# The recurrent mixer's inverses: the backward direction's U form in the other partition half, its products alternating with the forward's

## The reference

```python
def step(S, inp):
    r_t, w_t, k_t, v_t, kk_t, a_t = inp
    sa = jnp.einsum('dbhvk,dbhk->dbhv', S, kk_t)
    S = (S * w_t[..., None, :] - sa[..., :, None] * (kk_t * a_t)[..., None, :]
         + v_t[..., :, None] * k_t[..., None, :])
    return S, jnp.einsum('dbhvk,dbhk->dbhv', S, r_t)
_, ys = lax.scan(step, S0, seqs)
ys = jnp.moveaxis(ys, 0, 2)
y = ys[0] + jnp.flip(ys[1], axis=1)
```

## Time and profile before

| | us |
|---|---|
| median of 3 runs | 3585.34 |
| lowest, highest | 3580.81, 3586.29 |
| the profiled execution, its own time | 3579.05 |
| its span, first to last instruction | 3577.7 |
| TensorE busy | 3337.4 (93%) |
| VectorE busy | 1795.8 (50%) |
| ScalarE busy | 1114.4 (31%) |
| GpSimd busy | 267.2 (7%) |
| mean granted clock of TensorE | 0.972 |

### The profile page before, as it was taken

One profiled execution on the slowest core, in us unless ns is written; L12 is line 12 of the kernel. 1 busy time (PEld: TensorE's weight loads), 2 busy tenths in 40 slices (PEclk: granted clock), 3 DMA queues, 4 the chain that ended last, 5 costly groups with the idle time before them and its releaser, 6 DMA issues. The chain is left out here.

```text
span 3577.7 us, 55649 instructions
## 1 busy us (share of the span) xinstructions
PE 3337.4 (93%) x23830; PEld 2326.5 (65%) x23830; DVE 1795.8 (50%) x2790; ACT 1114.4 (31%) x1847; POOL 267.2 (7%) x218
## 2 busy tenths in 40 slices
PE   8989799998898997999989799889999999899999
PEld 6687543332667753333358688858888878688887
DVE  4655433322466443333245666476664562866735
ACT  3643300000355330000032433124333432743423
POOL 1011000000101100000020222301000100010001
PEclk9999999999999998999999899989999999999999
DMA  5131389999412217999962000012222222222222
GB/s 187 48 118 71 119 330 428 427 428 427 192 48 95 94 48 319 427 427 427 428 244 106 2 3 3 4 36 100 95 94 95 94 98 80 66 94 94 95 91 75
DMA packets 54389, 595.58 MB, mean 166 GB/s; under 512 B 5760, under 2 KB 10112, under 8 KB 16512
## 3 DMA queue, kind: packets, MB, share of 16 engines
q1 hardware_dynamic: 54144, 592.03, 41.2%
HBM read 589.91 MB, written 2.10 MB: 165 GB/s over the span
## 5 line engine op out<-in xcount | busy, mean ns | idle before, releaser
L683 PE MATMUL psum<-source_hi,weights_hi 128*128 128x512 f32 (+1 forms) x2352 | 922.6, 392 | 52.2 <-DVE weights_lo L570 36.4
L683 PE MATMUL psum<-source_lo,weights_hi 128*128 128x512 f32 (+1 forms) x2352 | 910.2, 387 | 0.0
L683 PE MATMUL psum<-source_hi,weights_lo 128*128 128x512 f32 (+1 forms) x2352 | 910.0, 387 | 0.0
L683 PEld LDWEIGHTS psum<-source_hi,weights_hi 128*128 128x128 f32 x2352 | 448.7, 191 | 154.8 <-DVE weights_lo L570 44.7
L570 DVE TENSOR_TENSOR weights_lo<-weight_ring,weights_hi 128x1024 fp32r<-128x1024 f32 (+4 forms) x321 | 350.8, 1100 | 320.3 <-ACT weights_hi L518 319.5
L683 PEld LDWEIGHTS psum<-source_lo,weights_hi 128*128 128x128 f32 x2352 | 448.9, 191 | 89.5 <-issue 3.4
L683 PEld LDWEIGHTS psum<-source_hi,weights_lo 128*128 128x128 f32 x2352 | 448.0, 190 | 88.5
L518 ACT CAST weights_hi<-weight_ring 128x1024 fp32r<-128x1024 f32 (+4 forms) x321 | 297.0, 935 | 614.0 <-PE psum L683 602.3
L1867 DVE TENSOR_TENSOR x<-psum,x 128x512 f32<-128x512 f32 x250 | 160.4, 684 | 207.2 <-PE psum L1714 207.2
L632 POOL TENSOR_TENSOR sums_of_squares<-squares 128x512 f32<-128x512 f32 (+1 forms) x17 | 27.7, 1629 | 2498.6 <-ACT squares L538 2498.6
L1678 PE MATMUL psum<-lent_weights,branches 128*64 128x512 f32 x800 | 182.1, 597 | 3.6 <-DMA lent_weights<-in_w_gate 2.5
(11 more groups left out here) (388 smaller groups left out, 4588.0 us busy)
## 6 DMA issues: line engine op xcount, KB each, us to landing
lent_weights<-in_w_down SPq DMA_DIRECT2D x26, 2048.0 KB, 18.5
lent_weights<-in_w_up SPq DMA_DIRECT2D x24, 2048.0 KB, 20.0
lent_weights<-in_w_gate SPq DMA_DIRECT2D x22, 2048.0 KB, 19.2
weight_ring<-in_ffn_w_up SPq DMA_DIRECT2D x22, 2048.0 KB, 7.7
weight_ring<-in_w_gate SPq DMA_DIRECT2D x20, 2048.0 KB, 16.3
weight_ring_first<-in_w_up SPq DMA_DIRECT2D x20, 2048.0 KB, 18.0
weight_ring<-in_w_up SPq DMA_DIRECT2D x16, 2048.0 KB, 20.8
weight_ring<-in_w_down SPq DMA_DIRECT2D x16, 2048.0 KB, 19.2
```

The lines of the kernel that those rows point to most:

```text
L683: ins = pe.matmul(ps, a, b, start=k == 0 and q == 0, stop=k == job.rows // P - 1 and q == 2)
```

## The change

Slots are renamed: U moves to slot `VAL`, Y and the early work's temporary to slot `GAMMA`. `far(d, h)` gives the partition half h for the forward direction and the other half for the backward one. The backward U, and the backward Y that belongs to it, now lie in the far half.

- Front: one more entry in `ops`, A's product again, written to the far half for the backward direction and copied through the mask of the first level; VectorE adds the identity, and that is U after level one. T's entry is masked with the first level at once, with the sign, and the identity added. `first_level` is gone.
- Inverses, TensorE: `together` issues a block of one direction and a block of the other, product by product; `alone` issues one block. T's update (forward) goes with Y's product (backward), and the next level's Y product (forward) with T's update (backward). U's updates stand alone. For the last level `move_back` makes the backward U in the near half: identity x U plus Y x U, accumulated in PSUM, which VectorE copies.
- Inverses, ScalarE: the last backward Y is copied with its sign turned; one `scale` of a level stands between the two copies.
- Inverses, VectorE: `mix` and `decay_sum` follow the updates of their direction, a level earlier than before.

```diff
 KAPPA, RHO, BETA, GAMMA, VAL, AT, BT, R1, R2, AM, VT, GT, BTT = range(13)
-T_INV, U_INV, Y_MAT = BETA, GAMMA, VAL
...
 I64, M_LT, M_GT, M_LE, M_GE, M_LEVEL = 0, 1, 2, 3, 4, 5
+M_FIRST = M_LEVEL, M_LEVEL + 6
...
+def far(d, h):
+
+    h = (h + d) % 2
+    return slice(HALF * h, HALF * h + HALF)
...
-        act.activation(self.w[d][:, VAL, :], self.x[d][:, XA, :], ACT.Identity, scale=self.col("rwkv_k_a_2"), bias=self.bias)\
+        act.activation(self.w[d][:, TEMP, :], self.x[d][:, XA, :], ACT.Identity, scale=self.col("rwkv_k_a_2"), bias=self.bias)\
...
@@ -2237,7 +2244,8 @@
     near = slice(0, HALF - 1), slice(1, HALF)
     edge = slice(0, 1), slice(HALF - 1, HALF)
 
-    ops = [(VT, None, None, None), (BTT, BETA, None, None), (AT, BETA, KAPPA, "strict"), (R1, BETA, RHO, "upto"),
+    ops = [(VT, None, None, None), (BTT, BETA, None, None), (AT, BETA, KAPPA, "strict"), (U_INV, BETA, KAPPA, "first"),
+           (R1, BETA, RHO, "upto"),
            (T_INV, KAPPA, BETA, "turned"), (GT, GAMMA, None, None), (BT, GAMMA, KAPPA, "strict"),
            (R2, GAMMA, RHO, "upto")]
     by_act = [kind is None for _, _, _, kind in ops]
@@ -2268,13 +2276,20 @@
                     r, s = slice(HALF * h, HALF * h + HALF), slice(n * HALF, (n + 1) * HALF)
                     lhs = val[d][r, s] if a is None else w[d][r, a, s]
                     rhs = w[d][r, b, s] if b is not None else c64(K, I64)[r, :]
-                    return pe.matmul(K.psum[r, 2 * (i % 4) + d, s], lhs, rhs, start=True, stop=True)
-
-                for n in range(NCH):
-                    op(0, 0, n)
-                    op(1, 1, n)
-                for n in range(NCH):
-                    last = op(0, 1, n), op(1, 0, n)
+                    to = far(d, h) if slot == U_INV else r
+                    return pe.matmul(K.psum[to, 2 * (i % 4) + d, s], lhs, rhs, start=True, stop=True)
+
+                if slot == U_INV:
+                    for n in range(NCH):
+                        op(0, 0, n)
+                        op(1, 0, n)
+                        last = op(0, 1, n), op(1, 1, n)
+                else:
+                    for n in range(NCH):
+                        op(0, 0, n)
+                        op(1, 1, n)
+                    for n in range(NCH):
+                        last = op(0, 1, n), op(1, 0, n)
                 for ins in last:
                     ins.then_inc(ready, 1)
 
@@ -2306,16 +2321,17 @@
                     if by_act[i]:
                         continue
                     dve.wait_ge(ready, 2 * i + d + 1)
-                    mask = {"strict": (M_LT, M_GT), "upto": (M_LE, M_GE), "turned": (M_GT, M_LT)}[kind][d]
-                    dve.scalar_tensor_tensor(out=chunks(w[d][:, Y_MAT if kind == "turned" else slot, :]),
-                                             in0=chunks(K.psum[:, 2 * (i % 4) + d, :]),
-                                             scalar=-1.0 if slot == R1 else 1.0, in1=over_chunks(c64(K, mask)),
+                    if slot == T_INV:
+                        dve.wait_ge(ready, 2 * i + 2)
+                    mask = {"strict": (M_LT, M_GT), "upto": (M_LE, M_GE), "turned": M_FIRST, "first": M_FIRST[::-1]}[kind][d]
+                    to = chunks(w[d][:, slot, :])
+                    dve.scalar_tensor_tensor(out=to, in0=chunks(K.psum[:, 2 * (i % 4) + d, :]),
+                                             scalar=-1.0 if slot in (R1, T_INV, U_INV) else 1.0, in1=over_chunks(c64(K, mask)),
                                              op0=ALU.mult, op1=ALU.mult).then_inc(kept, 1)
                     done += 1
-                    if kind == "turned":
+                    if slot in (T_INV, U_INV):
                         dve.wait_ge(kept, done)
-                        dve.wait_ge(ready, 2 * i + 2)
-                        link(first_level(K, dve, link, w[d], T_INV, Y_MAT))
+                        link(dve.tensor_tensor(to, to, over_chunks(c64(K, I64)), ALU.add))
 
...
+        near = lambda d, h: slice(HALF * h, HALF * h + HALF)
 
         @block.tensor
         def _(pe):
+
+            def of(d, bank, lhs, rhs, here, there):
+                def op(n, h):
+                    c = slice(n * HALF, (n + 1) * HALF)
+                    return pe.matmul(K.psum[there(d, h), bank + d, c], w[d][here(d, h), lhs, c], w[d][here(d, h), rhs, c],
+                                     start=True, stop=True)
+                return op
+
+            def y(d):
+                return of(d, 0, AM, T_INV, near, far)
+
+            def t(d):
+                return of(d, 4, U_INV, Y_MAT, far, near)
+
+            def u(d):
+                return of(d, 2, Y_MAT, U_INV, far, far)
+
+            def alone(op, sem):
+                for n in range(NCH):
+                    for h in range(2):
+                        ins = op(n, h)
+                ins.then_inc(sem, 1)
+
+            def together(op, sem, other, other_sem):
+                for n in range(NCH):
+                    op(n, 0)
+                    other(n, 0)
+                    last = op(n, 1), other(n, 1)
+                last[0].then_inc(sem, 1)
+                last[1].then_inc(other_sem, 1)
+
+            def move_back():
+                for n in range(NCH):
+                    c = slice(n * HALF, (n + 1) * HALF)
+                    for h in range(2):
+                        r, ps = far(1, h), K.psum[near(1, h), 3, c]
+                        pe.matmul(ps, c64(K, I64)[r, :], w[1][r, U_INV, c], start=True, stop=False)
+                        ins = pe.matmul(ps, w[1][r, Y_MAT, c], w[1][r, U_INV, c], start=False, stop=True)
+                ins.then_inc(u_upd, 1)
+
+            def await_level(m, d):
+                if m:
+                    pe.wait_ge(masked, 2 * (m - 1) + d + 1)
+                    pe.wait_ge(t_updated, 2 * (m - 1) + d + 1)
+
+            def await_y(m, d):
+                pe.wait_ge(y_kept, 2 * m + d + 1)
+                if m:
+                    pe.wait_ge(u_updated, 2 * (m - 1) + d + 1)
+
+            alone(y(0), y_ready)
             for m in range(levels):
-                for d in range(2):
-                    if m:
-                        pe.wait_ge(masked, 2 * (m - 1) + d + 1)
-                        pe.wait_ge(t_updated, 2 * (m - 1) + d + 1)
-                    heads(pe, d, 0, AM, T_INV, y_ready)
+                await_level(m, 1)
+                if m < levels - 1:
+                    await_y(m, 0)
+                    together(t(0), t_upd, y(1), y_ready)
+                else:
+                    alone(y(1), y_ready)
+                    await_y(m, 0)
+                alone(u(0), u_upd)
                 if early and m < 2:
                     if m:
                         pe.wait_ge(early.gates, 2)
                     early.low_rank(pe, m, 6)
-                for d in range(2):
-                    pe.wait_ge(y_kept, 2 * m + d + 1)
-                    if m:
-                        pe.wait_ge(u_updated, 2 * (m - 1) + d + 1)
-                    else:
-                        pe.wait_ge(u_begun, d + 1)
-                    if m < levels - 1:
-                        heads(pe, d, 4, U_INV, Y_MAT, t_upd)
-                    heads(pe, d, 2, Y_MAT, U_INV, u_upd)
+                await_y(m, 1)
+                if m < levels - 1:
+                    await_level(m + 1, 0)
+                    together(y(0), y_ready, t(1), t_upd)
+                if m < levels - 1:
+                    alone(u(1), u_upd)
+                else:
+                    move_back()
 
         @block.scalar
...
-                    act.copy(w[d][:, Y_MAT, :], K.psum[:, d, :]).then_inc(y_kept, 1)
+                    act.activation(w[d][:, Y_MAT, :], K.psum[:, d, :], ACT.Copy,
+                                   scale=-1.0 if d and m == levels - 1 else 1.0).then_inc(y_kept, 1)
+                    if early and m < 2 and d == 0:
+                        early.scale(act, 2 * m + 2)
                 if early and m < 2:
                     early.gate(act, m, 6)
-                    early.scale(act, 2 * m + 2)
                     early.scale(act, 2 * m + 3)
 
...
         def _(dve):
-            link = linker(dve, dlink)
-            for d in range(2):
-                first_level(K, dve, link, w[d], U_INV, AT).then_inc(u_begun, 1)
-            dve.wait_ge(u_begun, 2)
             for m in range(levels):
-                if early and m in (1, 2, 3):
-                    early.mix(dve, 2 * m - 2)
-                    early.mix(dve, 2 * m - 1)
-                if early and m in (2, 4):
-                    early.decay_sum(dve, m // 2 - 1)
                 for d in range(2):
                     if m < levels - 1:
                         dve.wait_ge(t_upd, 2 * m + d + 1)
                         dve.tensor_tensor(w[d][:, T_INV, :], w[d][:, T_INV, :], K.psum[:, 4 + d, :],
                                           ALU.subtract).then_inc(t_updated, 1)
                     dve.wait_ge(u_upd, 2 * m + d + 1)
+                    if d and m == levels - 1:
```

(10 more changed lines are left out.)

24 lines of the change are left out of this document (8 added, 16 removed).

## The result

The changed kernel takes 3589.0 us, the median of 19 runs (3582.9 to 3594.0), against 3581.4 for the kernel before (19 runs, 3576.4 to 3589.4): 1.0019 times as long, with a 95% interval of 1.0013 to 1.0026. The forecast was 3579, faster by 6.4; the kernel is slower by 7.6, and an unchanged time lies outside the interval.

A forecast was written before the change was run, and what follows sets the result against it. TensorE was taken to bound the inverses, where paired blocks would overlap fully. Last pass -4.9, three loaded passes -7.5 and four fronts +6.0 gave -6.4 us, so about 3579 us; range 3568 to 3600.

The forecast's parts named there:

- A pair costs a block, 0.933 us: Inverses: forward and backward blocks on four quarters overlap fully, 64 records in 0.933 us; 1.87 without further overlap.
- The last pass, 19 slots of 0.933 and some waits, 23.4 us: Last pass's inverses: 17.7 us of slots, 2.1 moving U back, 3.5 waits and ends; 4.9 us saved against 28.3.
- a floor per record: Rival for pairs in the inverses: 20 to 25 ns a record, 1.3 to 1.6 us a pair, total 3585 to 3593; chance 0.14.
- The loaded passes, 27.9 us: Inverses of the three passes with early work: 27.9 us against 30.4, 2.5 saved each, 7.5 together.
- its sign of being wrong: Forecast is wrong if pairs overlap but a loaded pass stays above 29.5 us, or the front loses over 2.
- The helpers' term: Loaded passes: ScalarE's late copies add 1.8 us, VectorE's mixes and decay sums 0.3, raising 25.8 to 27.9.
- The waits for ScalarE's copies in levels 1 and 2: Loaded passes: copies stand behind two gates and a scale, so TensorE waits about 0.9 us in each of two levels.
- The bound of 30.4: Upper bound for a loaded pass: VectorE's 27.35 busy us less four first-level operations, plus 6 us of waits.
- The front, 1.5 us: Each front ends 1.5 us later, bound by VectorE's added operations beside GpSimd; four times, 6.0 us lost.
- Moving the U form back, 2.1 us: End of a pass's inverses: last backward U update becomes 32 accumulated products, 64 records, taking 2.1 us.
- No fall of the clock to 1.2 GHz: TensorE's gaps stay near 1 us in a stage granted 1.00 throughout, so no clock fall was expected.

The follow-up runs named there:

- e6: Changed kernel plus two unread products of constants ending each front and state stage, keeping TensorE busy into the barriers; 3587.0 us, 1.0011 of the kernel before.
- e3: Changed kernel with three runs of 1024 instructions (unread products of constants) ahead of its last pass; one execution, 3623.0 us.
- e5: Kernel before with only the front's part: U form's first level made in the front, in its own half; 3590.5 us, 1.0028 of the kernel before.
- e7: e4 plus the unread products of constants ending each front and state stage; 3576.4 us, 0.9985 of the kernel before.
- e4: Kernel before with the change's helper order alone, and GpSimd's first mask held until VectorE's first levels; 3574.6 us, 0.9979 of the kernel before.
- e1: Changed kernel with the two blocks of a pair issued one after the other; 3591.4 us, 1.0026 of the kernel before.

## Why the prediction was wrong, step by step

- **A pair costs a block, 0.933 us: right**, 0.935 measured. The Trainium skill ("TensorE: Matmul & The Clock Gate", section "Part 3: Packing small matmuls") allows a weight load beside a running product only in another row group; the trace decided against it, as column halves in the earlier trace rows had said.
- **The last pass, 19 slots of 0.933 and some waits, 23.4 us: this step failed.** The price of one pair was right, but eight of them in a row ask for instructions at twice the rate at which the kernel gets them. The stage took 29.36. The six starts after stops are 0.6 to 1.3 us late, some 6.0 us together, and 29.4 - 6.0 = 23.4 is the forecast work. The prediction had named the hole itself (nothing showed 128 records and loads in a row at 7 ns each) and priced it as a floor per record, which is another mechanism: a floor would slow every pair, and a pair between two stops is not slow. The total of that rival, 3585 to 3593, fits; its pair of 1.3 to 1.6 us does not exist. That 3589 lies inside the range is owed to the width left for this rival, whose mechanism was wrong, and not to the sum.
- **The loaded passes, 27.9 us: wrong for the same reason.** At full clock this order took 30.54 in the changed kernel, 29.39, 28.96 and 30.51 in e6, and 29.43, 29.72 and 29.52 in e3: 29.7 on average against 30.72, 1.0 us saved and not 2.5, and above the 29.5 that the prediction named as its sign of being wrong. They seem to differ by where in a pass the stops fall. The helpers' term can't be read apart, since stops fell into the same waits. The waits for ScalarE's copies in levels 1 and 2 came as expected: starts 0.8 us late. (The profile's row at 2046.80 names GpSimd's mask, which ends just after the copy; the mask that this product needs is an earlier one.) The bound of 30.4 was mis-added: 27.35 less some 5 plus 6 is 28.4; nothing hangs on it.
- **The front, 1.5 us: nearly right**, 1.17. VectorE's additions beside GpSimd took 1.57 and 0.92 us, not 1.76 and 0.95, and its last masked copy ends 1.16 us later than before; TensorE's wait at the barrier is 1.96 us, not 2.3.
- **Moving the U form back, 2.1 us: slightly high.** its 64 records took 1.9 us.
- **"No fall of the clock to 1.2 GHz": wrong.** A state stage with 3.4 us at low clock took 30.13 us against 28.97 without, a front with 6.8 took 21.50 against 20.23. In the kernel before, the low stretches of the profiled execution fell on the start of a front and cost nothing: its first 64 records took 3.63 us (front at 2092.88) instead of 2.08 (front at 2250.39), but the next product waits for VectorE anyway (0.44 us instead of 1.99), and the front took 19.08 us either way.

**What the 7.6 us are.** By stages at full clock: fronts 4 x 1.17 = 4.7, last pass +0.8, loaded passes 3 x -1.0 = -3.0, together +2.5. In the profiled executions the mixer took 12.0 us more (318.92 against 306.89): these 2.5, 0.8 for the loaded pass that took 30.54 and not 29.7, and 8.8 in the five stages that low clock lengthened (2.3 and 2.8 in inverses, 1.3 and 1.3 in fronts, 1.2 in a state stage). But this execution was the longest of the 19, and its clock, 0.968, is below their mean of 0.9701.

The runs can be split in another way, which is an estimate. Each has its mean granted clock (for the kernel before I take the 44 runs that were timed beside the experiments); at 0.971 the changed kernel takes 3588.6 us (5 runs) and the kernel before 3584.6 (6), at 0.972 it is 3585.9 (3) and 3581.2 (16): 4 to 5 us slower at the same clock. The kernel before takes 3585.3 us at 0.970 (4 runs) and 3578.7 at 0.974 (9), 1.65 us for each 0.001; the changed kernel's mean clock is 0.9701 and that of before 0.9723, which is 3.6 us. 4.3 + 3.6 = 7.9 against the measured 7.6. So about half is the work and half goes with the clock; of the work, the 1.8 us between 2.5 and 4.3 are not traced to a stage. For e5 the same slope gives 2.7 us, and 7.3 + 2.7 is its 10. For e7 it fails: its clock is 0.0009 above that of e4, and it is slower.

What remains open is why the changed kernel is granted less. Its stops are not the reason: e1 shows none and has a mean clock of 0.9707, and e5, which has the front's part and only traces of stops, 0.9705. All three have the longer front; e6, with TensorE busy at its end, has 0.9724, about the value of before. That points to the front's end, but e6's gain in time is within its interval, and no run settles it. Nor is the supply theory's last link shown in full, that a packet holds just 256 instructions of TensorE's: it rests on the counts between stops, on the size and number of the packets and on their times. Why a packet takes that long to come no run shows.

## What to carry to other kernels

Before packing small products closer, divide: instructions of TensorE (weight loads and each pass of an fp32 product count) by the time that the packed stage is to take. In this kernel the packed stage got one every 13.6 to 16.4 ns, and after a few hundred instructions in store no faster; where the division comes out below that, expect the same stops; cut instructions (longer moving operands, as in e3) and not array time. When a rate taken from a short stretch is multiplied by a long one, look for what has to be refilled in between; and try the small reordering that a large change brings along by itself, since here it and one delayed operation of GpSimd gained 7 us where the whole change lost as much.

## What the runs showed of the hardware

- TensorE takes a weight load and a matmul of 64 x 64 by 64 columns every 14.6 ns when they walk the four quarters, for some 390 instructions; after that it gets 256 instructions in 3.47 us (a plain run of constants, e3) to 3.9 us on average (last pass of the changed kernel).
- A stop for instructions shows as idle with the releaser "issue", at equal counts of instructions (126 to 128 records) and not at the edges of blocks, and ends 2.3 to 2.7 us after a packet of instructions begins (e3, changed kernel).
- The two diagonal quarters ask for an instruction every 14.6 ns, which is as fast as they come: the kernel before had next to no slack there, and its profile gave no sign of it; in e5 the same products fell 0.5 us behind in two passes of four.
- A stretch of 3.4 us at 1.2 GHz cost 1.2 us in a state stage (30.13 against 28.97) and nothing at the start of a front, where TensorE's next product waits for VectorE (19.08 both ways).
- An operation of VectorE with both operands in SBUF takes 0.69 us alone and 1.57 to 1.76 when it runs wholly beside GpSimd; holding GpSimd's first mask back took 1.2 us from the last pass (e4).
